# Prompt attention with one score pass: row tiles, exponential with the row maximum as bias, probabilities turned by TensorE

## The reference, cut to what matters

```python
def fox_attend(q, k, v, cq, ck, q_pos, k_pos):
    s = jnp.einsum('bqhd,bkhd->bhqk', q, k).astype(jnp.float32) * (DH_A ** -0.5)
    s = s + jnp.transpose(cq, (0, 2, 1))[..., :, None] - jnp.transpose(ck, (0, 2, 1))[..., None, :]
    mask = k_pos[None, :] <= q_pos[:, None]
    s = jnp.where(mask, s, -jnp.inf)
    p = jax.nn.softmax(s, axis=-1)
    return jnp.einsum('bhqk,bkhd->bqhd', p.astype(v.dtype), v)
```

## Time and profile before

| What | us |
|---|---|
| median of three runs | 2280.24 (2278.18 to 2285.32) |
| the profiled execution | 2277.98 |
| its span, first to last instruction | 2276.2 |
| TensorE busy | 2227.5 (98%) |
| VectorE busy | 1165.6 (51%) |
| ScalarE busy | 788.3 (35%) |
| GpSimd busy | 428.7 (19%) |
| prompt attention, first score product to last value product | 185.36 to 351.58 |

### The profile page before, as it was taken

One profiled execution on the slowest core, in us unless ns is written; L12 is line 12 of the kernel. 1 busy time (PEld: TensorE's weight loads), 2 busy tenths in 40 slices (PEclk: granted clock), 3 DMA queues, 4 the chain that ended last, 5 costly groups with the idle time before them and its releaser, 6 DMA issues.

```text
span 2276.2 us, 33056 instructions
## 1 busy us (share of the span) xinstructions
PE 2227.5 (98%) x13655; PEld 2058.0 (90%) x13655; DVE 1165.6 (51%) x1611; ACT 788.3 (35%) x1206; POOL 428.7 (19%) x533
## 2 busy tenths in 40 slices
PE   8999999999999999999999999999999999999998
PEld 8997777799999999999999889999999998888887
DVE  2226762263636363111533478667676766556446
ACT  3124664242524253112221124444434345333321
POOL 0001123001011101000022122453545420001001
PEclk9999999999999999999999999999999999999999
DMA  5508645401212121311322222222222249445420
GB/s 165 207 20 233 178 125 181 142 22 40 77 40 77 38 79 38 112 47 52 98 72 95 93 102 59 79 71 77 75 73 75 74 126 321 171 130 173 149 83 38
DMA packets 202012, 233.53 MB, mean 103 GB/s; under 512 B 40634, under 2 KB 161702, under 8 KB 200182
## 3 DMA queue, kind: packets, MB, share of 16 engines
q1 hardware_dynamic: 192854, 201.54, 28.6%
q0 software_dynamic: 9008, 29.87, 4.0%
HBM read 167.75 MB, written 50.97 MB: 96 GB/s over the span
## 4 chain that ended last, share of the span: by engine, by line
PE 90%; DVE 3%; SPq 2%; issue 2%; ACT 1%; DMA 1%; POOL 1%; DVEq 0%; POOLq 0%; ACTq 0%
PE ps L688 43%; PE ps L1179 18%; PE ps L1203 11%; PE ps L1251 4%; PE ps L1101 3%; PE ps L1009 2%; PE ps L867 2%; PE ps L849 1%; SPq L2979 1%; PE ps L827 1%; DVE sb L1895 1%; PE ps L850 1%; PE ps L1060 1%; DVE sb L1999 0%; DMA kc<-k_lo 0%
## 5 line engine op out<-in xcount | busy, mean ns | idle before, releaser
L688 PE MATMUL ps<-x_hi,ring_hi 128*128 128x384 f32 x960 | 327.3, 341 | 3.0 <-ACT sb L1306 3.0
L688 PE MATMUL ps<-x_hi,ring_lo 128*128 128x384 f32 x960 | 321.6, 335 | 0.0
L688 PE MATMUL ps<-x_lo,ring_hi 128*128 128x384 f32 x960 | 321.5, 335 | 0.0
L1306 ACT ACTIVATE sb<-ps 128x512 f32<-128x512 f32 (+8 forms) x240 | 107.7, 471 | 359.0 <-PE ps L688 237.0
L688 PEld LDWEIGHTS ps<-x_hi,ring_hi 128*128 128x128 f32 x960 | 181.1, 189 | 6.5 <-issue 6.2
L1909 DVE TENSOR_TENSOR ring_lo<-ring_raw,ring_hi 128x1024 fp32r<-128x1024 f32 (+1 forms) x66 | 76.0, 1158 | 214.9 <-ACT ring_hi L1306 213.9
L688 PEld LDWEIGHTS ps<-x_lo,ring_hi 128*128 128x128 f32 x960 | 181.1, 189 | 0.9 <-issue 0.7
L688 PEld LDWEIGHTS ps<-x_hi,ring_lo 128*128 128x128 f32 x960 | 180.7, 188 | 0.0
L1203 PE MATMUL ps<-down_hi,h_hi 128*128 128x512 f32 x396 | 155.6, 393 | 0.2
L1203 PE MATMUL ps<-down_hi,h_lo 128*128 128x512 f32 x396 | 154.3, 390 | 0.0
L1203 PE MATMUL ps<-down_lo,h_hi 128*128 128x512 f32 x396 | 154.2, 389 | 0.0
(11 more groups left out here) (354 smaller groups left out, 5691.0 us busy)
## 6 DMA issues: line engine op xcount, KB each, us to landing
down_raw<-in_w_down SPq DMA_DIRECT2D x66, 512.0 KB, 3.7
ring_raw<-in_w_in SPq DMA_DIRECT2D x50, 512.0 KB, 3.9
h_raw<-h_chunks SPq DMA_DIRECT2D x66, 192.0 KB, 3.8
h_chunks<-convolved_halves SPq DMA_DIRECT2D x22, 512.0 KB, 2.8
up_raw<-in_w_up SPq DMA_DIRECT2D x37, 256.0 KB, 3.0
up_raw_b<-in_w_up SPq DMA_DIRECT2D x36, 256.0 KB, 3.8
sb<-in_x_prompt SPq DMA_DIRECT2D x16, 512.0 KB, 8.7
x_parts<-x_hi SPq DMA_DIRECT2D x3, 1536.0 KB, 9.1
```

What stands on the lines that cost most here:

```text
L688: m = mm(out, l, r, start=(n == 0), stop=(n == len(pairs) - 1))
L1306: return act.activation(out, in_, ACT.Copy, scale=scale)
```

## The change

Scores are made once, by query row tile (`row_scores(t)`, `t` over 64 tiles, 8 a head): tile `i` has all its (i+1) x 128 keys side by side, in one bank for `i < 4`, else in two. VectorE takes the maximum of the whole row and negates it (`row_max`); ScalarE's exponential reads PSUM with that column as its bias (`probs`). The result stands queries by keys, so TensorE turns it block by block (`turn_probs`) into one of two banks, in parts of up to four blocks; ScalarE copies the high part out of PSUM (`probs_hi`) and VectorE subtracts from PSUM (`probs_lo`). The value products go by query tile, each 128 wide. The row of the maxima, its transposes and its copies are gone, the rows of the operand sets that held it too, and there are two sets in place of three. Two tables say at which step of a head the scores and the exponential of a later tile are issued (8 to 11 are the next head's 0 to 3). The diff, cut to its core:

```diff
-        sets = [[rounded(f"{n}{i}", off[f"{n}{i}"], SEQ) for n in ("qq", "kk", "qc", "kc")] for i in range(3)]
+        sets = [[rounded(f"{n}{i}", off[f"{n}{i}"], SEQ) for n in ("qq", "kk", "qc", "kc")] for i in range(2)]
-        PL = [rounded(f"p_lo{i}", off[f"e{i}"], 1024) for i in range(3)]
+        PL = [rounded(f"p_lo{i}", off[f"pl{i}"], 1024) for i in range(3)]
...
+        NT_S = H_A * NP
+        SCORES_AT = {0: (4,), 2: (5,), 4: (6,), 5: (7,), 6: (8, 9), 7: (10, 11)}
+        EXPS_AT = {0: (3,), 1: (4,), 2: (5,), 4: (6,), 5: (7,), 6: (8, 9), 7: (10,)}
...
+        def row_scores_at(i):
+            return (bank[:, i] if i < 4 else ps[:, i % 2])[:, 0:(i + 1) * P]
+
+        def turned_parts(t):
+            h, i = divmod(t, NP)
+            m = 12 * h + (i if i < 4 else 2 * i - 4)
+            return [(m, 0, min(i, 3) + 1)] + ([(m + 1, 4, i + 1)] if i > 3 else [])
...
+            def row_scores(t):
+                h, i = divmod(t, NP)
+                if i == 0:
                     set_in(pe, h)
+                if h or i > 3:
+                    pe.wait_ge(s_ex, NP * h + (-1, -1, 0, 0, 2, 4, 5, 6)[i])
+                qq, kk, qc, kc = sets[h % 2]
+                o, q = row_scores_at(i), slice(i * P, (i + 1) * P)
+                for n, a, b in ROWS:
+                    if n != i:
+                        continue
+                    diag = b == (i + 1) * P
+                    mm(o[:, a:b], qq[:, q], kk[:, a:b], start=True, stop=False)
+                    m = mm(o[:, a:b], qc[0:KR, q], kc[0:KR, a:b], start=False, stop=not diag)
+                    if diag:
+                        m = mm(o[:, b - P:b], idr, causr, start=False, stop=True)
                 m.then_inc(s_p1, 1)
...
+            def turn_probs(t):
+                pe.wait_ge(s_ex, t + 1)
+                for m, j0, j1 in turned_parts(t):
+                    if m >= 2:
+                        pe.wait_ge(s_plo, m - 1)
+                    for j in range(j0, j1):
+                        ins = tr(bank[:, 4 + m % 2, (j - j0) * P:(j - j0 + 1) * P], E[t % 3][:, j * P:(j + 1) * P], ident)
+                    ins.then_inc(s_tp, 1)
...
+                pe.wait_ge(s_plo, parts_of(t))
+                o = bank[0:DH + 1, 6 + c, i % 4 * P:(i % 4 + 1) * P]
+                for j in range(i + 1):
+                    x = slice(j * P, (j + 1) * P)
                     for n, (v, p) in enumerate(split3(VH[h % 2], VL[h % 2], PH[t % 3], PL[t % 3])):
+                        m = mm(o, v[:, j, :], p[:, x], start=(j == n == 0), stop=(j == i and n == 2),
...
-            for u in range(NR):
-                row_scores(0, u)
-            for u in range(3):
-                row_scores(1, u)
-            turn_max(0)
-            for u in range(3, 6):
-                row_scores(1, u)
+            for t in range(4):
+                row_scores(t)
...
+            for t in range(NT_S + 1):
                 if t < NT_S:
+                    turn_probs(t)
+                    for n in at_step(SCORES_AT, t):
+                        row_scores(n)
+                else:
+                    past_keys(0, 0)
+                    past_keys(1, 1)
+                if t:
+                    probs_v(t - 1)
...
+            def probs(t):
+                act.wait_ge(s_mx, t + 1)
+                if t >= 3:
+                    act.wait_ge(s_tp, parts_of(t - 3))
+                i = t % NP
+                act.activation(E[t % 3][:, 0:(i + 1) * P], row_scores_at(i), ACT.Exp, bias=row_nm[:, t % 4:t % 4 + 1])\
+                    .then_inc(s_ex, 1)
+
+            def probs_hi(t):
+                if t >= 3:
+                    act.wait_ge(s_pv, t - 2)
+                for m, j0, j1 in turned_parts(t):
+                    act.wait_ge(s_tp, m + 1)
+                    copy(PH[t % 3][:, j0 * P:j1 * P], bank[:, 4 + m % 2, 0:(j1 - j0) * P]).then_inc(s_ph, 1)
+
+            for t in range(3):
+                probs(t)
+            for t in range(NT_S + 1):
+                h, i = divmod(t, NP)
                 if t < NT_S:
+                    probs_hi(t)
+                    for n in at_step(EXPS_AT, t):
+                        probs(n)
+                    if i == 1 and h:
+                        chunk_out(h - 1, 1)
+                    if i == 3 and h + 1 < H_A:
                         v_hi(h + 1)
+                    if i == 5:
+                        chunk_out(h, 0)
+                    if i == 6 and h % 2 == 0 and h + 2 < H_A:
+                        qk_hi((h + 2) // 2)
...
+            def row_max(t):
+                q = slice(t % 4, t % 4 + 1)
+                dve.wait_ge(s_p1, t + 1)
+                link(dve.tensor_reduce(row_mx[:, q], row_scores_at(t % NP), AX.X, ALU.max))
+                dve.tensor_scalar(row_nm[:, q], row_mx[:, q], -1.0, None, ALU.mult).then_inc(s_mx, 1)
...
+                for m, j0, j1 in turned_parts(t):
+                    dve.wait_ge(s_ph, m + 1)
+                    x = slice(j0 * P, j1 * P)
+                    dve.tensor_tensor(PL[t % 3][:, x], bank[:, 4 + m % 2, 0:(j1 - j0) * P], PH[t % 3][:, x].bitcast(F32),
+                                      ALU.subtract).then_inc(s_plo, 1)
...
             qk_lo(0)
             v_lo(0)
+            for t in range(4):
+                row_max(t)
             for t in range(NT_S):
+                h, i = divmod(t, NP)
                 probs_lo(t)
+                for n in at_step(SCORES_AT, t):
+                    row_max(n)
+                if i == 3 and h + 1 < H_A:
                     v_lo(h + 1)
+                if i == 7 and h % 2 == 0 and h + 2 < H_A:
+                    qk_lo((h + 2) // 2)
...
-            for i in range(3):
-                pool.wait_ge(s_pz, 4 * i + 4)
+            for i in range(2):
+                pool.wait_ge(s_pz, 4 + i)
                 past_pe(pool, ("va", 1, 3 * i + 2))
-                pool.memset(sets[i][2][64:P, :].bitcast(F32), 0.0).then_inc(s_pz, 1)
-                pool.memset(sets[i][3][64:P, :].bitcast(F32), 0.0).then_inc(s_pz, 1)
...
                 pool.memset(sets[i][2][64:66, :].bitcast(F32), 1.0).then_inc(s_pz, 1)
-                pool.memset(sets[i][3][96:98, :].bitcast(F32), 1.0).then_inc(s_pz, 1)
...
-                if "h" in parts and h >= 3:
-                    sp.wait_ge(s_s2, NS * (h - 2))
+                if "h" in parts and h >= 2:
+                    sp.wait_ge(s_p1, NP * (h - 1))
...
-            head_operands(2)
...
-                if g and g + 2 < H_A:
+                if g + 2 < H_A:
                     head_operands(g + 2)
```

More of the change, by code:

```diff
@@ L145, in build @@
         place(off["R1"], ("qq0", SEQ), ("kk0", SEQ), ("qc0", SEQ), ("qq1", SEQ), ("kk1", SEQ), ("qc1", SEQ),
[L146 to L147 removed]
+              ("e2", 1024), ("ph2", 1024), ("e0", 1024))
+        place(off["R2"], ("kc0", SEQ), ("qhi", SEQ), ("khi", SEQ), ("kc1", SEQ), ("pl0", 1024), ("pl1", 1024),
               ("e1", 1024), ("ph0", 1024), ("ph1", 1024))
[L149 removed]
+        off["pl2"] = off["kT"]
         off["om"], off["sP"], off["sPT"], off["oas"] = off["kT"], off["kT"] + 2 * T, off["kT"] + 3 * T, off["ost"]
@@ L273, in build @@
         rbb = at(off["kT"] + T, 1024)
-        mparts, mhl = at(off["mparts"], 2, NP), rounded("m_hi_lo", off["mhl"], NP, 2)
+        row_mx, row_nm = at(off["mparts"], 4), at(off["mparts"] + 4, 4)
         ost = at(off["ost"], 512)
@@ L572, in build @@
         s_lo = sem("qk_lo_ready")
[L573 to L579, removed]
+        s_set = [sem(f"operands_in{i}") for i in range(2)]
+        s_p1 = sem("row_scores_full")
+        s_mx = sem("row_max_or_x1_centred")
+        s_tp = sem("probs_turned")
         s_ex = sem("probs_ready")
@@ L657, in build @@
         ROWS = [(i, c, min((i + 1) * P, c + 512)) for i in range(NP) for c in range(0, (i + 1) * P, 512)]
[L658 to L663, removed]
+        NT_S = H_A * NP
+        SCORES_AT = {0: (4,), 2: (5,), 4: (6,), 5: (7,), 6: (8, 9), 7: (10, 11)}
+        EXPS_AT = {0: (3,), 1: (4,), 2: (5,), 4: (6,), 5: (7,), 6: (8, 9), 7: (10,)}
+        KR = 66
         LAST = NC_FF - 1
@@ L669, in build, with at_step, parts_of @@
         QB_EARLY = {DEC_B: 2, DEC_B + 1: 1}
[L671 to L676, removed]
+        def at_step(table, t):
+            h, i = divmod(t, NP)
+            return [NP * h + n for n in table.get(i, ()) if NP * h + n < NT_S]
+        def row_scores_at(i):
[4 more added lines that the diff above has]
+            return [(m, 0, min(i, 3) + 1)] + ([(m + 1, 4, i + 1)] if i > 3 else [])
+        def parts_of(t):
+            return turned_parts(t)[-1][0] + 1
         def set_in(eng, h):
-            eng.wait_ge(s_set[h % 3], 128 * (h // 3 + 1))
+            eng.wait_ge(s_set[h % 2], 128 * (h // 2 + 1))
         @block.tensor
@@ L857, in probs_v @@
-                c = int(s >= 2)
-                if s == 0:
+                h, i = divmod(t, NP)
+                c = i // 4
+                if i == 0:
                     pe.wait_ge(s_vl, h + 1)
-                if s in (0, 2) and h:
```

(18 more changed lines are left out.)

121 lines of the change are left out of this document (18 added, 103 removed).

## The result

The changed kernel takes 2309.47 us (median of 4 runs, 2304.93 to 2312.14); the kernel before, run beside it, 2279.21 (4 runs). The ratio is 1.0131, 95% interval [1.0108, 1.0154]: slower by 1.3%, and 1.5 us over the forecast of 2308. The profiled execution of after took 2304.93 us, with a span of 2303.1; that of before was 2277.98.

A forecast was written before the change was run, and what follows sets the result against it. TensorE, nearly full before, would give way to the order of ScalarE and VectorE in prompt attention: +20.4 us for the stage and +7 for the clock on 2277.98 make 2305.4, as a median 2308; range 2287 to 2336.

The forecast's parts named there:

- E(n) behind M(n) behind L(t) behind H(t): Steps 2, 4 to 7: ScalarE's exponential waits VectorE's negated maximum, queued behind its subtraction, which waits ScalarE's copy.
- the ring: Copy, subtraction, maximum, exponential, next copy: one loop through ScalarE and VectorE, hardly overlapping; 21.3 us a head against 19.6.
- Predicted +27.4: Prompt attention stage: 20.4 us longer from the summed heads, plus 7 for the clock, added to the profiled 2277.98.
- Ring's start: Lead-in of the stage: shrinks, so the loop starts at 189.1 where today's heads start at 198.51, 9.4 us in hand.
- Plain head 21.3: Heads 1, 3, 5 and 6, without a query/key split: 21.3 us each, summed over the eight steps.
- Query/key split +4.05: Heads 0, 2 and 4: two ScalarE copies (1.9 us) and two VectorE subtractions (2.15) in the way, 4.05 us more.
- The clock +7: TensorE's pauses lower its clock to 1.2 GHz at times: 0.9 us a head, 7 us in all.
- Head 7 21.9: Last head of the stage, to the end of its last values: 21.9 us, with no next tiles.
- Operand sets "at nothing": Two operand sets in place of three, eight transfers a head as before: wanted over 15 us later, so no cost.
- A: Rival, faster: TensorE stays the bound and gets 2.3 us lighter a head, 16.8 us a head, 2252; chance 0.08.
- C: Rival: TensorE's clock low for much of the stage, 20.4 + 24 us, so 2325; chance 0.11.
- D: Rival: narrow value products 0.109 us apart instead of 0.06, +14 us, so 2322; chance 0.09.

The follow-up runs named there:

- e2_busy: The kernel after, with 12 more turns and 18 more value products per head on TensorE, repeated into the same result: 2302.31 us, ratio 1.0116.
- e4_pool_apart: The kernel after, with GpSimd's pair multiplication of heads 4 and 6 held until VectorE's v_lo subtraction of that pair is done: 2304.72 us, ratio 1.0126.
- e5_qk_spread: The kernel after, with a pair's query/key split cut in four: query copy and subtraction at step 2, key's at step 4: 2296.28 us, ratio 1.0087.

## Why the prediction was right, point by point

**The mechanism.** The forecast rested on E(n) behind M(n) behind L(t) behind H(t). The idle times are ended by whom it named (78.6 us by the negation, 65.0 by the copy, 2.0 by TensorE), TensorE is busy for 77% of the stage (about three quarters was asked for), and the edits that open the ring or lighten it move the time, while the lighter maximum and the spread split do nothing once it is open.

**The stage.** Predicted +27.4. Measured: from the first score product at 184.66 to 378.13, where the last value product hands over, 193.5 us, against 166.2 before: +27.3. That it agrees to 0.1 us is partly luck; the terms do not:

- Ring's start, 3.7 us after the first score product: 188.11, so 3.45 after 184.66. Right in sum, but the terms listed for it come to 3.0; the 0.69 us from the first score product to the start of VectorE's remainder at 185.35 are not among them.
- Plain head 21.3: heads 3 and 5 took 21.21 and 21.18. Right. Its prices held as well: in the groups of after M is 0.81 at 640 columns, 1.08 at 896 and 1.22 at 1024 (taken: 0.82, 1.09, 1.22), E 0.90, 1.01 and 1.12 at 768, 896 and 1024 (0.90, 1.01, 1.11), H and L at 512 0.59 and 0.69 (0.60, 0.69).
- Query/key split +4.05: head 2 stands 4.7 over a plain head, head 4 without the contention 4.35. Too small by about 0.5, three times.
- The clock +7: mis-sized. Heads at 0.92 took as long as one at 1.00, so the 0.9 a head was about 0. Only head 1 clearly paid, 1.5 us by e2_busy; there the level stayed at 1.2 GHz for some 6.8 us, twice as long as in head 3 below. Its window:

```profile
220.90:227.70 6.80, 6.40 (x31) 5.82 (x32) 4.01 (x8) 2.71 (x6) 0.00 (x0) 0.51 0.73 276
```

- Head 7 21.9: from its first copy at 354.51 to 378.13 it took 23.6. The turns of the past keys were overlooked; they stand between the last turns and the last value products, as they did before. The chain in order of time:

```profile
374.91 1.77 PE ps L876 x16
376.68 1.45 PE ps L856 x24
```

- Operand sets "at nothing": in head 0 VectorE waited for the transfers of the first two heads' sets before it wrote tile 2's low part, since that buffer lies where head 1's transfer was still reading the keys' low half. The prediction had not placed this on VectorE's path. Of that wait 1.06 us reached the ring (from the copy before it to E(768): 3.22 us, against 2.16 in head 3). The timeline of VectorE:

```profile
191.93 0.56 DVE L1986 TENSOR_TENSOR p_lo<-ps,p_hi 128x384 fp32r<-128x384 f32 x1 [1.98 <-DMA kc<-k_lo]
```

- The contention of VectorE and GpSimd, 2.1 us in heads 4 and 6, was not foreseen.

From the ring's start to the end the forecast without its clock term had 182.9 us; it took 190.0. The terms found make 1.4 (split) + 1.5 (clock) + 1.7 (head 7) + 1.1 (transfer) + 2.1 (contention) = 7.8 for a gap of 7.1. So the clock term of 7 was some 5.5 too large, and four smaller omissions (6.3 together) filled its place by chance; had they been absent, the forecast would have been 5 to 6 us too long.

**The rivals.** A (TensorE the bound, 2252) failed in this kernel for the reason given against it; with the ring open it came close, at 2258, and with plain heads of 16.6 to 16.9 where A had 16.8. C's sum was too high by its own figures: heads of 24.7 outlast the four plain ones of 21.3 by 3.4 each, but not the three with a split (24.9 and 25.4), so it comes to some 14, not 24. C fell all the same: the clock did drop after pauses, but came back. Windows of after behind two pauses of TensorE, which end at 259.20 (1.65 us) and 263.86 (1.89 us), each for VectorE's subtraction:

```profile
259.20:262.00 2.80, 2.76 (x32) 2.43 (x32) 2.68 (x6) 1.43 (x3) 0.00 (x0) 1.00 0.64 133
...
265.40:268.70 3.30, 3.25 (x23) 2.81 (x22) 1.57 (x3) 1.62 (x4) 1.61 (x3) 0.52 0.97 185
```

Behind the first pause the work ran at 2.4 GHz; behind the second the level fell to 1.2 GHz, stayed there for some 3.3 us of full work, and rose; over the stage the granted clock was 0.92. Rival C's oscillation (the Trainium skill, TensorE: Matmul & The Clock Gate, section HAM oscillation — how this bites in real kernels), in which every burst begins cold, did not show. The kernel of which this section of the Trainium skill tells waited for some 3 to 5 us each time, longer than the pauses here, so this case does not speak against the section, only against its use in rival C. D fell too. The timeline of TensorE in after, two neighbours in the last run of 24 value products:

```profile
377.86 0.22 PE L856 MATMUL ps<-p_lo,v_hi 128*65 128x128 f32 x1
377.91 0.22 PE L856 MATMUL ps<-p_hi,v_lo 128*65 128x128 f32 x1
```

They start 0.06 us apart, 1.45 us for 24, as in the earlier trace rows. The 81 ns that the Trainium skill gives for sustained products of 128 columns (TensorE: Matmul & The Clock Gate, section Back-to-back issue gap) are not what these products, with weights of 65 columns, take.

## What to carry to other kernels

When two engines hand each other work in turn, write down for each step what every instruction waits for and what is queued in front of that: if the chain closes on itself, durations add, however idle the engines look, and neither engine's busy share warns of it. The remedy is order, not speed: issue the producer one step ahead of its consumer; here one line was worth 51 us, more than the change had cost. Once the ring is open, price the next bound again, because an edit that was worth 27 us in the ring was worth nothing outside it, and waits that the ring had hidden (an operand's transfer) come up.

## What the runs showed that was not expected

VectorE's subtraction of 128x512 with both operands and its result in SBUF, 0.68 us alone, took 1.80 and 2.09 us beside GpSimd's 128x1024 multiplication in SBUF. No view shows it as a wait; it appears only as a group's mean, 999 ns, against 681 in e4_pool_apart:

```profile
L1970 DVE TENSOR_TENSOR v_lo<-sb,v_hi 128x512 fp32r<-128x512 f32 x8 | 8.0, 999 | 6.7 <-ACT v_hi L1284 6.7
```

Whenever it began beside it, it ended 0.54 to 0.55 us after the multiplication did (292.47 and 293.01; 340.38 and 340.93), and so it did where it took 2.22 us in e5_qk_spread (287.97 and 288.51): it looks like standing still until the other is done and then running, rather than like two engines at half speed. The Trainium skill (SBUF — State Buffer, section SBUF: two separate sides) tells of one pair of ports that VectorE, with two inputs in SBUF, and GpSimd take in turn, each for a whole instruction. The trace agrees, by these three pairs of times, and by the edit that kept the two apart. In e5_qk_spread it was GpSimd that came second, and its multiplication took 3.24 us instead of 2.37 while VectorE's subtraction kept its 1.23:

```profile
284.51 1.23 DVE L1967 TENSOR_TENSOR q_lo<-sb,q_hi 128x1024 fp32r<-128x1024 f32 x1 [1.28 <-ACT q_hi L1284]
284.73 3.24 POOL L2690 TENSOR_TENSOR sb<-sb 128x1024 f32<-128x1024 f32 x1 [2.18 <-DMA sb<-row_scales]
```

More work on TensorE raised its clock at no cost: 30 more products a head (e2_busy) took five of seven heads from below 1 to 1.00, and the kernel got no slower.
